# GpSimd takes its low part of a weight in four instructions of 512 columns instead of one of 2048

## The reference

```
# first block, per layer
h = rmsnorm(x); proj = h @ w_in            # split into HGRN2 and NSA inputs
o = [hgrn2_mixer(...), nsa_mixer(...)]     # recurrence; compressed, selected and window attention
x = x + rmsnorm(o @ w_out)
# second block, per layer
x = x + 0.5 * rmsnorm(swiglu(rms_norm(x), w13, w2))          # w13: 1024 x 5632, w2: 2816 x 1024
x = x + rms_norm(token_mixing(rms_norm(x), w_in, ...))       # retention, MLA, differential attention
x = x + rms_norm(cross_attention(rms_norm(x), mem, ...))
x = x + 0.5 * rms_norm(swiglu(...))                          # a second such pair of weights
```

## Time and profile before

| | |
|---|---|
| runs | 2408.93, 2409.20, 2406.36 us; median 2408.93 |
| profiled execution | 2408.86 us, its span 2407.1 us |
| TensorE (PE) | busy 2184.2 us, 12,707 matmuls |
| VectorE (DVE) | busy 1307.0 us, 1,587 instructions |
| ScalarE (ACT) | busy 1020.1 us |
| GpSimd (POOL) | busy 637.0 us, 221 instructions, of which 110 low parts |
| granted TensorE clock, mean | 0.958 |

### The profile page before, as it was taken

The page is one execution under the profiler, slowest core; times in us unless marked ns, Lnnn a source line. Parts: engine busy times, 40 slices in busy tenths (PEclk is TensorE's granted clock), DMA queues, the critical chain, the costliest instruction groups (busy, mean ns, idle before and its releaser), DMA issues.

```text
span 2407.1 us, 29682 instructions
## 1 busy us (share of the span) xinstructions
PE 2184.2 (91%) x12707; PEld 1913.3 (79%) x12707; DVE 1307.0 (54%) x1587; ACT 1020.1 (42%) x1334; POOL 637.0 (26%) x221
## 2 busy tenths in 40 slices
PE   6889997889878899889979999999998998998998
PEld 5878876878766799768768879979986877787997
DVE  4555675645665544555666455355445556745433
ACT  4434543424433444344535444334433454443442
POOL 2113242212233223222223222323322123222221
PEclk9989998999888999999999999999999999999999
DMA  6253233443222455343444445546553345442652
GB/s 241 89 164 119 88 123 105 133 160 108 85 83 84 166 191 177 131 155 123 162 149 145 156 140 181 187 149 207 181 180 128 116 158 175 146 160 97 210 190 100
DMA packets 190971, 351.59 MB, mean 146 GB/s; under 512 B 8124, under 2 KB 84984, under 8 KB 190840
## 3 DMA queue, kind: packets, MB, share of 16 engines
q1 hardware_dynamic: 189400, 344.46, 42.6%
q0 software_dynamic: 1440, 5.24, 0.6%
HBM read 348.63 MB, written 1.05 MB: 145 GB/s over the span
## 4 chain that ended last, share of the span: by engine, by line
PE 74%; DVE 14%; ACT 5%; issue 3%; POOL 2%; DMA 1%; SPq 0%; POOLq 0%; DVEq 0%; ACTq 0%
PE bank L1786 13%; PE bank L1792 13%; PE bank L1782 13%; PE bank L1812 7%; PE bank L1806 7%; PE bank L1809 7%; PE bank L1830 3%; DVE raw_r L2243 3%; PE bank L1847 2%; PE bank L1950 2%; ACT high L2055 2%; DVE units_r L2260 1%; PE bank L1821 1%; PE bank L1868 1%; POOL stat L2710 1%
## 5 line engine op out<-in xcount | busy, mean ns | idle before, releaser
L2721 POOL TENSOR_TENSOR raw_r<-raw,high 128x2048 fp32r<-128x2048 f32 (+2 forms) x110 | 545.0, 4955 | 1316.4 <-ACT high L2055 1316.4
L1782 PE MATMUL bank<-high,units_r 128*128 128x512 f32 (+1 forms) x1696 | 686.7, 405 | 45.5 <-ACT units_r L2072 19.2
L1786 PE MATMUL bank<-high,units_r 128*128 128x512 f32 (+1 forms) x1696 | 674.5, 398 | 25.2 <-DVE units_r L2260 25.1
L2055 ACT ACTIVATE high<-raw 128x2048 fp32r<-128x2048 f32 (+1 forms) x314 | 590.8, 1894 | 247.5 <-PE bank L1792 212.7
L2243 DVE TENSOR_TENSOR raw_r<-raw,high 128x2048 fp32r<-128x2048 f32 (+1 forms) x204 | 522.0, 2568 | 123.4 <-ACT high L2055 123.4
L1792 PE MATMUL bank<-raw_r,units_r 128*128 128x512 f32 (+1 forms) x1696 | 463.6, 396 | 22.7 <-DVE raw_r L2243 22.6
L1782 PEld LDWEIGHTS bank<-high,units_r 128*128 128x128 f32 x1696 | 326.1, 192 | 116.0 <-issue 40.2
L1806 PE MATMUL bank<-units_r,high 128*128 128x256 f32 x1600 | 403.6, 288 | 0.0
L1786 PEld LDWEIGHTS bank<-high,units_r 128*128 128x128 f32 x1696 | 325.6, 192 | 96.8 <-DVE units_r L2260 33.1
L1792 PEld LDWEIGHTS bank<-raw_r,units_r 128*128 128x128 f32 x1696 | 324.9, 192 | 94.3 <-DVE raw_r L2243 25.4
L1809 PE MATMUL bank<-units_r,high 128*128 128x256 f32 x1600 | 399.6, 285 | 0.0
(11 more groups left out here) (229 smaller groups left out, 1881.7 us busy)
## 6 DMA issues: line engine op xcount, KB each, us to landing
raw<-in_ffn_w_dram SPq DMA_DIRECT2D x132, 1024.0 KB, 5.1
raw<-in_w_in_dram SPq DMA_DIRECT2D x108, 1024.0 KB, 5.0
raw<-in_w_out_dram SPq DMA_DIRECT2D x24, 1024.0 KB, 5.0
raw<-in_cross_wkv_dram SPq DMA_DIRECT2D x16, 1024.0 KB, 5.1
raw<-in_w_branch_dram SPq DMA_DIRECT2D x12, 1024.0 KB, 4.8
raw<-in_cross_wq_dram SPq DMA_DIRECT2D x8, 1024.0 KB, 5.1
raw<-in_cross_wo_dram SPq DMA_DIRECT2D x8, 1024.0 KB, 5.0
raw<-in_w_in_dram SPq DMA_DIRECT2D x4, 832.0 KB, 4.4
```

Of the source, the lines that this page charges most:

```text
L1782: pe.matmul(o, h.high(k0 + k)[:, span], w[:, k, :], start=start and k == 0, stop=False, skip_group_check=True)
L1786: pe.matmul(o, h.low(k0 + k)[:, span], w[:, k, :], start=False, stop=False, skip_group_check=True)
L2055: act.activation(high, p.raw, ACT.Copy).then_inc(*mark(s.whigh, ("whigh", p.i)))
L2721: pool.tensor_tensor(low, p.raw, high.bitcast(F32), ALU.subtract).then_inc(*mark(s.wlow_p, ("wlow", p.i)))
```

## The change

Where GpSimd takes a low part, it now issues four subtractions of a quarter of the columns each, one after another, with no wait between them. The quarters cover the same columns (4 x 512 for a full piece; 4 x 416 and 4 x 48 for the three smaller ones). The wait ahead of them and the one signal behind the last of them are as before. VectorE's own low parts, the order of the steps and all else are unchanged.

```
     def split_low(p, low, high, by, **_):
         if by == "pool":
             hold.wait_ge(*at(("whigh", p.i)))
-            pool.tensor_tensor(low, p.raw, high.bitcast(F32), ALU.subtract).then_inc(*mark(s.wlow_p, ("wlow", p.i)))
+            n = low.shape[1] // 4
+            for c in range(4):
+                part = slice(c * n, c * n + n)
+                done = pool.tensor_tensor(low[:, part], p.raw[:, part], high[:, part].bitcast(F32), ALU.subtract)
+            done.then_inc(*mark(s.wlow_p, ("wlow", p.i)))
```

## The result

The changed kernel takes 2415.65 us, median of ten runs (2410.02 to 2419.89), against 2408.83 for the kernel before in the same series: ratio 1.0029, 95% interval 1.0018 to 1.0039. It is 0.3% slower. A second series gave 2414.11 against 2407.69, ratio 1.0026 (1.0016 to 1.0036). The forecast was 2395, faster, in a range of 2378 to 2413: wrong in sign, and just outside the range. The profiled execution's span is 2414.0 us, 6.9 over before.

What follows compares the result with a forecast made beforehand. TensorE, with 74% of the chain of waits, was taken as the bound, some VectorE holds by GpSimd's low parts leaving it idle. -18.0 - 4.5 + 8.5 = -14.0 us from 2408.86 gave 2395, range 2378 to 2413.

Steps and rivals of the forecast that it cites:

- (a): Where GpSimd's low part holds VectorE and TensorE idles behind: the hold lasts a quarter, not the whole; 18.0 us gained.
- The price of a quarter: GpSimd's 512-column subtraction: 1280 ns from a line through two measured sizes, so +0.4 us per low part.
- one quarter to 365.2: VectorE's L2571, held at 363.61, waits one quarter only; 3.0 us gained there, 1.8 at 767.05.
- my first rival: VectorE gets no turn between queued quarters, so every hold grows 0.4 us: 2414 us, chance 8%.
- The eight seams between GpSimd instructions: Further places in the trace with GpSimd instructions back to back; VectorE had the turn in each.
- (c): What gets later: low parts TensorE waits close behind, powers, level sums, norm at three seams; 8.5 us lost.
- Waits to the second quarter's end: At 1409.22, L2260 waits until 1410.2 instead of 1412.3: 2.2 us gained.
- (b): TensorE's half-clock stretches behind waits near 1409, 366 and 319 may go: 4.5 us gained, bounds 0 and 6.3.
- The 0.8 for powers and 1.8 for level sums: Losses in us where the norm's power (twice) or level sums starting the recurrence follow a GpSimd low part.
- The second rival: VectorE enters at all three seams in a low part, TensorE waits at its third pass: 2420 us, chance 10%.
- the 15 that was to be its sign: TensorE's waits for GpSimd's low-part line adding up to over 15 us would show late low parts.
- The fourth, given back: Most shrunken waits are followed by another for a chain that did not shrink: 2407 us, chance 22%.

Runs made afterwards that it cites:

- five cuts: Against the kernel before, only five of GpSimd's 110 low parts cut in four (near 310, 622, 659, 1241, 2040 us): 2394.21 us, ratio 0.9947.
- ten put back: Changed kernel with ten low parts whole again, six behind which TensorE waited and four at the seams: 2395.51 us, ratio 0.9952 to the kernel before.

## Why the prediction was wrong

Three steps failed: VectorE's turn at 363 and 767, the half clock that was to go with the shortened wait, at the seams, and the price of a late low part.

**The starting point was right.** That a VectorE instruction lay still for as long as GpSimd's low part, and that this cost TensorE time at a few places, is shown: five cuts gave -13.6 us. For the places of (a) other than 363, 767, 1409 and 2213 the forecast was 10.4 us and the trace has 11.6 (1.7, 1.7, 1.7, 3.5, 3.0; the third is 1.4 if read to 670 us only). At 2213 it was 0.6, in a stretch that gave 0.9, and 1.3 in two of the three kernels that cut low part 100 and not 99.

**The price of a quarter was right:** 1.28 forecast, 1.30 measured. A low part takes 4.93 to 5.07 us instead of 4.52 to 4.62.

**(a) failed at 363 and 767**, "one quarter to 365.2": -4.8 forecast, +1.1 and -0.1 measured, 5.8 off. VectorE got no turn there. That is my first rival, at two places only, with a condition that I had not seen: a gain load issued by GpSimd right ahead. The eight seams between GpSimd instructions that I had counted had none. The trace of before had a sign of it: L2571 starts 0.33 us ahead of the low part at 363.61 and loses all the same. I read over that as a race.

**(a) failed at 1409 and (c) at the three other seams.** "Waits to the second quarter's end" was right for the instruction: TensorE's wait for L2260 fell from 3.1 to 1.1. But I took that as kept at 1409 because no wait for the norm stood in the trace behind it. There was none only because TensorE's half clock had filled that time. -2.2 forecast, +1.8 measured. For the three others the forecast was 0.6 lost and, in the last one's stretch, 0.6 gained at 2213; measured +1.5, +1.3 and -0.9. Together 5.9 off. At 1800 it is not the low part alone: with low part 82 whole and the rest cut the place cost 1.2 all the same, and a half clock of 3.4 us lay on it, as in the changed kernel, that before has not.

**(b) failed at the seam:** 3.0 of its 6.3 stood there. The half-speed stretch did not go, it moved behind the next wait, where it costs. I priced the drop in the stretch where it stood, and not what waits at that stretch's end. Even gone, it is worth less than 3.0: in the kernel where no half clock lies between 1340 and 1440 (ten put back) the place gave 0.8. Behind 366 the wait did not shrink. Behind 319 the forecast was not wrong, only uncertain. Before, and in the kernel with five cuts:

```profile
323.00:326.40 3.40, 3.40 (x12) 0.50 0.00 0
```
```profile
318.00:324.00 6.00, 5.49 (x32) 1.00 0.09 36
```

The half clock is there in the changed kernel's first trace (-1.7) and in all kernels with low part 12 whole; in its second trace and the seven others with low part 12 in quarters or eighths it is gone, and they give -3.2 to -3.9. In the first trace, of the 4.5 forecast, nothing came: TensorE is busy 2185.7 us, before 2184.2.

**(c) was under-sized for the late low parts:** 5.3 forecast (2.3, 1.8, 1.2), at five places 9.5 measured, with 1.0 more at 27 us where TensorE now waits 1.4: 5.2 off. I let one VectorE low part in between and forgot the two L2260 that follow it, each of which also goes ahead of a quarter: at 401 the low part took 9.3 us instead of 6.3. At 1300 two VectorE low parts went in, and a slack of 2.9 that (c) had left out was gone: 10.9 us instead of 6.4.

Set right, -14.0 + 5.8 + 5.9 + 4.5 + 5.2 - 1.2 comes to +6.2, and with the 1.6 at 1376, which stands in no term, to +7.8, where the span shows +6.9. The 0.8 for powers and 1.8 for level sums are left in it as forecast; no run takes them apart. That it fits so well is partly luck, as single stretches move by microseconds from run to run. The second rival named the mechanism that weighs most, at 10%, and priced it for twelve low parts: six were enough, with the seams, and TensorE's waits for L2724 stayed at 10.6 us, under the 15 that was to be its sign. The fourth, given back, holds at the seams.

## What to carry to other kernels

Cutting an instruction that keeps another engine out shortens the wait of that engine and lengthens its own finish by whatever is let in between; so list, for each instance, what the one waits for and what slack the other has, and cut only where the first is on the path. A wait that shrinks is worth what the next wait does not take back, and a stretch at half clock that ends at a wait costs little (0.8 us here of about 3) until the work in it is sped up and the half clock moves behind the wait. Seven cuts out of 110 and one moved DMA were worth 1.0%; all 110 cost 0.3%.

## What was not expected of the hardware

A DMA issued by GpSimd right ahead of its tensor instructions kept VectorE's instruction, with two SBUF inputs, out through up to four of them back to back: 5.8 us with quarters, 5.5 with halves, against 1.4 and 0.7 with the DMA issued by SyncE. The Trainium skill, SBUF — State Buffer, Who interferes with whom, names the read interface for such an instruction and infers that descriptor generation needs only the write interface; by that the load should not matter to L2571. In this trace it does.

TensorE's granted clock fell to 0.50, the 1.2 GHz level, at 1411.9 before and at 1419.7 after, during a wait of 3.1 and of 3.7 us, and not with the one of 1.1 us at 1410.7: 23 matmuls in the 5.5 us after that, all at 1.00.
